# Hybrid decoder block with a top-4-of-32 expert stage: residual tiles loaded during the last item, its rows finished apart

## The reference

```
h = rmsnorm(x); proj = h @ w_mix_in          # conv, diff-attention and memory groups
x = x + concat(groups) @ w_mix_out
h = rmsnorm(x)
top_logit, top_idx = top_k(h @ router_w + router_b, 4); gates = softmax(top_logit)
for each expert e, for its tokens:
    gate, up = split(h[tok] @ w_gate_up[e] + b_gate_up[e])
    act = (clip(up, -7, 7) + 1) * (min(gate, 7) * sigmoid(1.702 * min(gate, 7)))
    y = (act @ w_down[e] + b_down[e]) * gate_of_token
x = x + sum of the y of each token's 4 experts
out = rmsnorm(x) * final_norm_g
```

## Time and profile before

| what | us |
|---|---|
| median of 3 runs | 2342.4 |
| lowest and highest run | 2339.67, 2343.84 |
| the profiled execution's own time | 2346.0 |
| its span, first to last instruction | 2344.4 |
| start of PE on the first item | 631.8 |
| end of PE on the last item | 2309.2 |
| last store issued | 2337.9 |

### The profile page before, as it was taken

How to read it: one execution, slowest core, us unless ns; L and a number is a source line. 1 busy time by engine, 2 the same in 40 slices (tenths; PEclk the granted TensorE clock), 3 DMA queues, 4 the chain that set the end, 5 groups by cost and what they waited for, 6 DMA issues and landing times.

```text
span 2344.4 us, 34502 instructions
## 1 busy us (share of the span) xinstructions
PE 2175.7 (93%) x10770; PEld 1797.6 (77%) x10771; DVE 1559.5 (67%) x1640; ACT 1337.9 (57%) x1523; POOL 341.2 (15%) x306
## 2 busy tenths in 40 slices
PE   7999868799499999999999999999999999999993
PEld 6889645599388878877887878778888878888873
DVE  4411256655577658677866888987666888667754
ACT  5111247733366557566746777775556777556654
POOL 1000000012302002011201122121221222122100
PEclk9999979999699999999999999999999999999997
DMA  5111200052679669689968999997776999667854
GB/s 192 55 54 54 90 1 1 25 192 100 200 233 324 218 190 379 229 287 319 379 215 288 361 359 370 362 372 251 226 239 227 322 371 358 222 222 249 302 161 161
DMA packets 265288, 536.93 MB, mean 229 GB/s; under 512 B 14478, under 2 KB 31144, under 8 KB 265132
## 3 DMA queue, kind: packets, MB, share of 16 engines
q1 hardware_dynamic: 248332, 488.26, 58.8%
q0 software_dynamic: 16896, 47.83, 8.4%
HBM read 499.29 MB, written 36.75 MB: 229 GB/s over the span
## 4 chain that ended last, share of the span: by engine, by line
PE 69%; issue 7%; DVE 6%; ACT 3%; DMA 1%; POOL 0%; DVEq 0%; ACTq 0%; SPq 0%; POOLq 0%
PE ps L686 65%; ACT hT_hi L1146 1%; PE ps L911 1%; PE ps L918 1%; DVE work L1400 1%; PE ps L832 1%; DVE hT_lo L1565 1%; DVE w_lo L1554 1%; ACT region_mem L1181 0%; DVE work L1605 0%; DVE hT_lo L1575 0%; ACT hT_lo L1194 0%; DVE weight_ring L1681 0%; DVE slots_between L1554 0%; DVE d_lam L1397 0%
## 5 line engine op out<-in xcount | busy, mean ns | idle before, releaser
L686 PE MATMUL ps<-hT_hi,hT_lo 128*128 128x512 f32 (+1 forms) x4304 | 1399.1, 389 | 12.4 <-DVE hT_lo L1575 12.4
L686 PEld LDWEIGHTS ps<-hT_hi,hT_lo 128*128 128x128 f32 x4304 | 808.5, 189 | 183.3 <-DVE w_lo L1554 18.3
L1146 ACT ACTIVATE hT_hi<-weight_ring 128x2048 fp32r<-128x2048 f32 x417 | 786.9, 1914 | 195.7 <-PE ps L686 142.0
L1554 DVE TENSOR_TENSOR slots_between<-weight_ring,hT_hi 128x2048 fp32r<-128x2048 f32 x245 | 552.7, 2285 | 140.3 <-ACT hT_hi L1146 139.7
L686 PE MATMUL ps<-slots_between,hT_lo 128*128 128x512 f32 x1344 | 527.1, 392 | 0.0
L1554 DVE TENSOR_TENSOR w_lo<-weight_ring,hT_hi 128x2048 fp32r<-128x2048 f32 x140 | 319.5, 2283 | 33.7 <-ACT hT_hi L1146 33.7
L686 PE MATMUL ps<-w_lo,hT_lo 128*128 128x512 f32 (+1 forms) x896 | 336.1, 375 | 0.0
L686 PEld LDWEIGHTS ps<-slots_between,hT_lo 128*128 128x128 f32 x1344 | 254.4, 189 | 54.2
L686 PEld LDWEIGHTS ps<-w_lo,hT_lo 128*128 128x128 f32 x896 | 168.7, 188 | 30.3
L607 POOL DMA_INDIRECT residual_rows<-work,idx_now x48 | 119.0, 2478 | 475.7 <-ACT work L1207 284.8
L601 POOL DMA_INDIRECT work<-normed_rows,idx_far x49 | 86.7, 1770 | 457.4 <-PE ps L911 293.8
(11 more groups left out here) (251 smaller groups left out, 2468.4 us busy)
## 6 DMA issues: line engine op xcount, KB each, us to landing
weight_ring<-in_w_gate_up SPq DMA_DIRECT2D x280, 1024.0 KB, 7.3
weight_ring<-in_w_down SPq DMA_DIRECT2D x140, 1024.0 KB, 5.6
weight_ring<-in_w_mix_in SPq DMA_DIRECT2D x10, 1024.0 KB, 5.9
weight_ring<-in_x SPq DMA_DIRECT2D x8, 512.0 KB, 8.0
weight_ring<-in_w_mix_out SPq DMA_DIRECT2D x4, 1024.0 KB, 5.3
work<-in_x SPq DMA_DIRECT2D x8, 512.0 KB, 4.7
residual_rows<-work SPq DMA_DIRECT2D x8, 512.0 KB, 3.3
normed_rows<-work SPq DMA_DIRECT2D x8, 512.0 KB, 3.6
```

The source lines that it names most:

```text
L686: return pe.matmul(o, l, r, start=first, stop=last)
L1146: act.activation(w_high_part(u), ring[:, home(u), :], ACT.Copy).then_inc(s["w_high_made"], 1)
L1554: dve.tensor_tensor(w_low_part(u), ring[:, home(u), :], w_high_part(u).bitcast(f32), ALU.subtract)\
```

## The change

SP issues the 8 tile loads and the gain load inside the loop, at the last item: each waits until POOL has signalled `earlier_added` and PE has used the unit whose slot it overwrites. The gain is the ninth load. POOL signals `earlier_added` when it comes to the last item, so the tiles hold the sums of all items but the last. ACT squares tiles 0 to 3 between units 9 and 10 of the last item and tiles 4 to 7 after a_high 1, with one root for four tiles; DVE normalises them at the matching places, and SP stores all 1024 rows. POOL meanwhile gathers the residual rows of the last item's tokens (the rows as they were before it) into `xg`. When `y_rows` stands, DVE adds the two, ACT and DVE normalise these rows on chip, and POOL scatters them over `out` once all eight stores have landed. The last item's adding scatter is gone.

The diff, cut to its core:

```diff
 SHORT = P // 2
+FINAL_GAIN_UNIT = 4
+FINAL_EARLY, FINAL_LATE = range(0, 4), range(4, S // P)
...
-            return ring[:, t // 2, D * (t % 2):D * (t % 2) + D]
+            return ring[:, home(t // 2), D * (t % 2):D * (t % 2) + D]
+        def final_gain():
+            return ring[:, home(FINAL_GAIN_UNIT), 0:D]
+        def final_junk():
+            return ring[:, home(FINAL_GAIN_UNIT), D:2 * D]
...
             with sp.Fori(0, MAX_ITEMS // GROUP) as group:
-                size_group = sp.value_load(table[2:3, bass.ds(group * GROUP + 2, 1)], min_val=0, max_val=CAP + 1)
+                size_group = sp.value_load(table[2:3, bass.ds(group * GROUP + 1, 1)], min_val=0, max_val=CAP + 1)
...
-            sp.wait_ge(s["all_added"], 1)
-            for t in range(NT):
-                sp.dma_start(final_tile(t), acc_d[P * t:P * t + P, :]).then_inc(s_final[t], 16)
-                if t == 0:
-                    sp.dma_start(wk[:, 5, :], a["final_norm_g"].partition_broadcast(P)).then_inc(s_gf, 16)
+                        with sp.Else():
+                            now = sp.value_load(table[2:3, bass.ds(k + 1, 1)], min_val=0, max_val=CAP + 1)
+                            with sp.If(now > 0):
+                                sp.wait_ge(s["earlier_added"], 1)
+                                for t in range(NT):
+                                    sp.wait_ge(s["w_used"], k * 12 + (HI_SLOTS + t // 2 + 1))
+                                    sp.dma_start(final_tile(t), acc_d[P * t:P * t + P, :]).then_inc(s_final[t], 16)
+                                sp.wait_ge(s["w_used"], k * 12 + (HI_SLOTS + FINAL_GAIN_UNIT + 1))
+                                sp.dma_start(final_gain(), a["final_norm_g"].partition_broadcast(P)).then_inc(s_gf, 16)
...
+            def rows_gather(b, kind="full"):
+                rows = rows_of(kind)
+                pool.indirect_dma_start(
+                    xg[rows, b, :], None, acc_d[:, :],
+                    bass.IndirectOffsetOnAxis(ap=idx_now.bitcast(i32)[rows, b, 0:1], axis=0)).then_inc(s_rows_in[b], 16)
+            def rows_scatter(b, kind="full"):
+                rows = rows_of(kind)
+                pool.indirect_dma_start(
+                    out[0, :, :], bass.IndirectOffsetOnAxis(ap=idx_now.bitcast(i32)[rows, b, 0:1], axis=0),
+                    y_rows[rows, b, :], None, bounds_check=S - 1, oob_is_err=False).then_inc(s_rows_out[b], 16)
...
-                            pool.wait_ge(s["y_made"], it * 2 + 3)
-                            pool.sem_inc(s["pool_waited"], 1)
-                            scatter(0)
-                            pool.wait_ge(s_scatter[0], it * 16 + 32)
-                            pool.sem_inc(s["pool_waited"], 1)
-                            by_second(pool, size_now, lambda kind: scatter(1, kind),
-                                      lambda: pool.dma_start(nothing[0:1, 1, :], ident[0:1, 0:16]).then_inc(s_scatter[1], 16))
-                            pool.wait_ge(s_scatter[1], it * 16 + 32)
-                            pool.sem_inc(s["pool_waited"], 1)
 ...
+                                pool.wait_ge(s["y_made"], it * 2 + 3)
+                                pool.sem_inc(s["pool_waited"], 1)
+                                scatter(0)
+                                pool.wait_ge(s_scatter[0], it * 16 + 32)
+                                pool.sem_inc(s["pool_waited"], 1)
+                                by_second(pool, size_now, lambda kind: scatter(1, kind),
+                                          lambda: pool.dma_start(nothing[0:1, 1, :], ident[0:1, 0:16]).then_inc(s_scatter[1], 16))
+                                pool.wait_ge(s_scatter[1], it * 16 + 32)
+                                pool.sem_inc(s["pool_waited"], 1)
...
                             with pool.Else():
-                                pool.sem_inc(s["all_added"], 1)
+                                pool.sem_inc(s["earlier_added"], 1)
+                                for b in range(BLOCKS):
+                                    pool.wait_ge(s_xturned[b], it + 1)
+                                pool.sem_inc(s["pool_waited"], 1)
+                                rows_gather(0)
+                                by_second(pool, size_now, lambda kind: rows_gather(1, kind),
+                                          lambda: pool.dma_start(nothing[0:1, 0, :], ident[0:1, 0:16]).then_inc(s_rows_in[1], 16))
+                                pool.wait_ge(s["rows_made"], 1)
+                                pool.wait_ge(s_fout, 16 * NT)
+                                pool.sem_inc(s["pool_waited"], 1)
+                                rows_scatter(0)
+                                by_second(pool, size_now, lambda kind: rows_scatter(1, kind),
+                                          lambda: pool.dma_start(nothing[0:1, 1, :], ident[0:1, 0:16]).then_inc(s_rows_out[1], 16))
+                                for b in range(BLOCKS):
+                                    pool.wait_ge(s_rows_out[b], 16)
...
+            def final_squares(n, tiles):
+                act.wait_ge(s_gf, 16)
+                for t in tiles:
+                    act.wait_ge(s_final[t], 16)
+                    act.wait_ge(s["act_chain"], 18 + t)
+                    act.activation(final_junk(), final_tile(t), ACT.Square, accum_out=e_ssq[:, t:t + 1]).then_inc(s["act_chain"], 1)
+                act.wait_ge(s["act_chain"], 18 + tiles[-1] + 1)
+                cols = slice(tiles[0], tiles[-1] + 1)
+                act.activation(e_std[:, cols], e_ssq[:, cols], ACT.Sqrt, scale=1.0 / D, bias=eps[:, :]).then_inc(s_fsq, 1)
+            def rows_std_of(kinds):
+                act.wait_ge(s["act_chain"], 18 + NT)
+                for b, kind in enumerate(kinds):
+                    act.wait_ge(s["rows_summed"], b + 1)
+                    rows = rows_of(kind)
+                    act.activation(final_junk()[rows, :], xg[rows, b, :], ACT.Square, accum_out=rows_ssq[rows, b:b + 1])\
+                        .then_inc(s["rows_squared"], 1)
+                    act.wait_ge(s["rows_squared"], b + 1)
+                    act.activation(rows_std[rows, b:b + 1], rows_ssq[rows, b:b + 1], ACT.Sqrt, scale=1.0 / D, bias=eps[rows, :])\
+                        .then_inc(s["rows_std"], 1)
...
                     x_high(0, it + 1, "full")
+                with act.Else():
+                    final_squares(0, FINAL_EARLY)
...
                     high_unit(it + 1, 2)
+                with act.Else():
+                    final_squares(1, FINAL_LATE)
 ...
+                with act.If(size_next < 1):
+                    rows_std_of(kinds)
...
-            for t in range(NT):
-                act.wait_ge(s_final[t], 16)
-                act.activation(wk[:, 4, :], final_tile(t), ACT.Square, accum_out=e_ssq[:, t:t + 1]).then_inc(s["act_chain"], 1)
-                act.wait_ge(s["act_chain"], 18 + t + 1)
-                act.activation(e_std[:, t:t + 1], e_ssq[:, t:t + 1], ACT.Sqrt, scale=1.0 / D, bias=eps[:, :]).then_inc(s_fsq, 1)
...
+            def final_norms(n, tiles):
+                dve.wait_ge(s_fsq, n + 1)
+                cols = slice(tiles[0], tiles[-1] + 1)
+                dve.reciprocal(e_rstd[:, cols], e_std[:, cols]).then_inc(s["final_rstd"], 1)
+                dve.wait_ge(s["final_rstd"], n + 1)
+                for t in tiles:
+                    dve.scalar_tensor_tensor(out=final_tile(t), in0=final_tile(t), scalar=e_rstd[:, t:t + 1], in1=final_gain(),
+                                             op0=ALU.mult, op1=ALU.mult).then_inc(s_fdone, 1)
+            def rows_finished(it, kinds):
+                dve.wait_ge(s["y_made"], it * 2 + 3)
+                for b, kind in enumerate(kinds):
+                    rows = rows_of(kind)
+                    dve.wait_ge(s_rows_in[b], 16)
+                    dve.tensor_tensor(xg[rows, b, :], y_rows[rows, b, :], xg[rows, b, :], ALU.add).then_inc(s["rows_summed"], 1)
+                for b, kind in enumerate(kinds):
+                    rows = rows_of(kind)
+                    dve.wait_ge(s["rows_std"], b + 1)
+                    dve.wait_ge(s["rows_summed"], b + 1)
+                    dve.reciprocal(rows_rstd[rows, b:b + 1], rows_std[rows, b:b + 1]).then_inc(s["rows_rstd"], 1)
+                    dve.wait_ge(s["rows_rstd"], b + 1)
+                    ins = dve.scalar_tensor_tensor(out=y_rows[rows, b, :], in0=xg[rows, b, :], scalar=rows_rstd[rows, b:b + 1],
+                                                   in1=final_gain()[rows, :], op0=ALU.mult, op1=ALU.mult)
+                ins.then_inc(s["rows_made"], 1)
...
                     dve.sem_inc(s_xlow[0], 1)
+                    final_norms(0, FINAL_EARLY)
...
                     dve.sem_inc(s["sum_made"], 6)
+                with dve.If(size_next < 1):
+                    final_norms(1, FINAL_LATE)
+                    rows_finished(it, kinds)
...
-            dve.wait_ge(s_gf, 16)
-            for t in range(NT):
```

(11 more changed lines are left out.)

## The result

The changed kernel took 2642.9 us (median of 4 runs, 2637.9 to 2647.4) against 2343.1 us before in the same runs: ratio 1.1276, 95% interval 1.1249 to 1.1304. It is slower by 300 us where I had forecast 20. The sign was right; the size was not, and neither was my account of where most of the time would go.

The account below looks back on a forecast made before the run. The prediction took PE to bound the expert stage, with 35 us behind it where nothing overlaps. Part 1's +9 and Part 2's +10.6 made 19.6 on 2342.4: 2362 us, range 2348 to 2380.

Parts of the forecast that it names:

- part 1: All items: four table loads on ACT in each delay units 3 and 10; +9 us, bounds 0 and 25.
- From there to unit 3 it was 2.13: ACT, one-block boundary: from results 1's start to unit 3, 2.13 us of loop scalar work, 2.2 with another branch.
- rival 2: ACT, all items: a table load holds ACT for twice its row, 1.28 us more each; 2428 us, 5%.
- rival 3: The table loads in the items are hidden, Part 2 as worked; 2353 us, 12%.
- The forecast wait of 0.4 at unit 3: One-block items: PE stalls 0.4 us at unit 3 for DVE's low part, about 14 times.
- Part 2: Last item and end: the serial tail goes, PE ends 19 us later, 27 us of rows and exit follow; +10.6 us.
- rival 4: Program end: as forecast, but POOL's DRAIN behind the last landing is short; 2356 us, 15%.
- 1: ACT's idle time takes all table loads and squares, PE ends at 2309.2 as before; 2333 us, 5%.
- 5: Last item: tiles land so late that the work runs serially, last store or scatter later; 2370 us, 8%.

Follow-up runs that it names:

- fit_both: The changed kernel with 91 increments ahead of ACT's item loop and 49 ahead of DVE's, branched over once: 2360.2 us, ratio 1.0060.
- act_97: The kernel before with 96 increments at the end of ACT's item loop, run only in the last item: 2391.6 us.
- roots_only: The kernel before with small roots in three last-item branches on ACT, so the changed kernel's table loads stand in every item: 2347.6 us, ratio 1.0012.
- squares_later: rows_behind with ACT copying units 10 and 11 before squaring tiles, and the gain load, second roots and DVE's products later: 2338.5 us, ratio 0.9965.
- Border_76: fit_both with 75 increments instead of 91 ahead of ACT's item loop, which then begins at 700: 2746.3 us.
- rows_behind: fit_both with POOL's scatter of block 0's finished rows moved behind its item loop: 2349.6 us, ratio 1.0023.

## Why the prediction was wrong

**The step that failed** is in part 1: "From there to unit 3 it was 2.13, the scalar work of the loop; with one more branch 2.2". I counted what the branches and increments of the new last-item code take to run and took the loop's own scalar work over unchanged. But that code is in each of the three copies of the item, skipped or not, and it pushed both loops over a fourth block. At the boundary shown above the 2.2 became 10.2 us: from results 1, which began at 1619.9 as the second of that pair, to unit 3 at 1631.3, less the load of 1.28. The measured size of the missed term is 283 us: after against fit_both. The warning was in the length of the compiled loops, which I didn't hold against anything. The Trainium skill says it as well (Runtime: NRT & Kernel Launch, Instruction fetch mechanics): a taken branch to a page outside the two that are held waits for a DMA fetch. I had not weighed it. Its sizes don't fit here, though: with two pages of 256 instructions ACT's loop at 728-1092 could be held, if every second border counts from the 960 that act_97 shows (704, 960, 1216), and it isn't; the packets are of 128. The runs decide: three blocks of 128.

I had also named a one-block item that is 2 us longer as the mark of rival 2, the table load that holds ACT twice. It was over 10 longer, and the mark was of something that none of my rivals held. A sign that several causes can give is no test.

**Part 1 without fetches** was 9; roots_only gives 2.7 (-1 to 6), in rival 3's direction, which had it at 0. The forecast wait of 0.4 at unit 3 doesn't exist: in fit_both PE's row for it is missing. ACT's timeline there shows why:

```profile
1472.70 1.28 ACT L1254 ACT_TABLE_LOAD   x1
1474.00 1.27 ACT L1254 ACTIVATE work<-ps,idx_now 128x512 f32<-128x512 f32 x2
1475.82 1.28 ACT L1193 ACT_TABLE_LOAD   x1 [0.55 <-issue]
```

The first load didn't push results 1 and then 2.1 of scalar work; results 1 had waited for PE and no longer did, and the queue did its scalar work under the two activations, so 0.55 is left of it. Unit 3 is late by 1.5 and not by 2.45, less than its low part had to spare. At unit 10 PE's 15 waits went from 12.4 to 13.7: 0.09 each, against 0.1. Table loads of 1.28 are right, and so is that no drain goes with them (the next activation starts 0.02 behind): rival 2 is refuted.

**Part 2** held nearly to the end, as fit_both shows with its loops held and its last item at the times of the old trace (ACT's unit 8 at 2291.9 against 2292.04):

```profile
2307.24 1.06 ACT L1264 ACTIVATE weight_ring<-weight_ring 128x1024 f32<-128x1024 f32 x1 [11.59 <-DMA weight_ring<-in_final_norm_g]
...
2312.12 1.28 ACT L1267 ACT_TABLE_LOAD   x1
...
2315.03 3.71 ACT L1193 ACTIVATE hT_hi<-weight_ring 128x2048 fp32r<-128x2048 f32 x2
...
2329.28 0.69 ACT L1254 ACTIVATE work<-ps,idx_now 128x512 f32<-128x512 f32 x1 [0.62 <-PE ps L733]
```

The gain at 2307.2 (forecast 2306.6), units 10 and 11 copied at 2318.7 (2318.0), results 1 at 2329.3 (2328.8), the rows' product at 2336.2 (2335.6). Then the scatter, which only writes, landed in 3.2 where I took 6.2 from the adding one; 3.6 had been my lower bound, and just missed. The turns of POOL's loop took 6.5 (6.05) and the DRAIN 6.1 (5.96), so rival 4 is out. The sum is +9.3 in the spans, against +10.6. In the timed runs fit_both is 14.8 above before; the two parts by themselves make 12. So the forecast of 2362 describes the changed kernel as it would be at another address, 2360.2, and not the kernel that was to be predicted.

**Rivals.** 1 is refuted by the 11.6 us wait, though squares_later shows that what it described can be had. 5 didn't occur. In the changed kernel itself the last item has the wait for the gain, 10.5 us, and the DRAIN as well; from PE's start on the last item to the end of the span it takes 81 us where the kernel before took 73, so some 8 of its 300, though unit 3 waits there too.

**What stays open.** Where the engine's three blocks come from (four, of which one is filled ahead, would be a reading), and whether GpSimd, SyncE and PE have the same bound: no loop of theirs was varied. Border_76, with three holes on ACT (13 us where shown) and none on DVE, is 104 us slower than the changed kernel, with two on ACT (10) and three on DVE (14 where shown). All of it lies in PE's wait for the low part at unit 3, 327.0 us against 223.3; why holes on ACT cost PE more there than holes on DVE wasn't tried.

## What to carry to other kernels

Code that a loop only skips still has to lie somewhere: count the instructions between a loop's head and its jump on every engine, all copies together, before counting what they take, and keep rare work behind the loop. By the rule found here, which was tested on ACT and DVE with loops of 221 to 364 instructions, a loop of up to 257 fits three blocks of 128 wherever it begins (127 and 257 make 384); up to 384 it fits only from the right address, and an unrelated edit ahead of it can make or break it. Holes that end in "issue" right behind a branch, with packets on the queue of instruction fetches all through the run, are its mark; and where two engines stand at once, mending one shows nothing in the time, so look in the trace for what it did.

## What the runs showed of the hardware

- A fetch at a jump on ScalarE or VectorE costs 4.1 to 5.8 us, as the medians by run and kind of jump go (2.4 to 2.8 at ACT's jumps into two-block copies), and up to 4.7 once more in border_76, where the target lies 4 instructions ahead of a border.
- What is held goes by address: the same loop of 335 instructions cost 47 us at 624-959 and 267 us at 674-1009.
- The table loads of 1.28 us, some 140 of them, cost 2.7 us in all (-1 to 6) in roots_only, where ACT's timeline has room.
- GpSimd's DRAIN at the end of the program took 5.96 us in the kernel before, 6 us behind its last landed transfer, and 6.12 in rows_behind, 0.2 behind it.
